# Two-block layer: block transfers on SyncE's queue, y read piece by piece, the keys and values projected in the stage before, the attention loop written out

## The reference, cut to what matters

```
first_block:  h = rmsnorm(x)*(1+scale)+shift;  u = h @ w_in
              y = concat(gated_delta(u[:4128], 8 heads of 128, chunks of 64, both directions),
                         rwkv7(u[4128:], 16 heads of 64, both directions))
              x = rmsnorm(x + gate*(y @ w_out))
second_block: h = x*(1+scale)+shift; q,k,v,g_attn,glu_a,glu_b,g_conv = split(h @ w_in_2)
              y_attn = banded_sink_attention(q,k,v)*silu(g_attn)     # window 128, 16 query, 4 kv heads
              y_conv = conformer_conv(glu_a,glu_b)*silu(g_conv)      # 31 taps deep, depthwise
              x = layer_norm(alpha*x + gate*(concat(y_attn,y_conv) @ w_out_2))
```

## Time and profile before

| | |
|---|---|
| times of three runs | 4370.04, 4384.80, 4388.81 us (median 4384.8) |
| profiled execution | 4372.03 us, span 4370.1 us |
| PE busy | 3557.6 us (81%), mean granted clock 0.902 |
| DVE, ACT, POOL busy | 2135.4, 1060.3, 824.6 us |
| DMA | 375768 packets, 464.6 MB; 230368 packets under 512 B |

### The profile page before, as it was taken

The page is one execution under the profiler, slowest core; times in us unless marked ns, Lnnn a source line. Parts: engine busy times, 40 slices in busy tenths (PEclk is TensorE's granted clock), DMA queues, the critical chain, the costliest instruction groups (busy, mean ns, idle before and its releaser), DMA issues. The chain is left out here.

```text
span 4370.1 us, 54075 instructions
## 1 busy us (share of the span) xinstructions
PE 3557.6 (81%) x19810; PEld 2969.9 (68%) x19810; DVE 2135.4 (49%) x4046; ACT 1060.3 (24%) x1764; POOL 824.6 (19%) x589
## 2 busy tenths in 40 slices
PE   7749999989995877778878777784977787778697
PEld 2238888878885777777777677783766676556385
DVE  0253555555553566566565546664020866681202
ACT  1123555533331112112122112221011221111102
POOL 0000000000000111111111100000655555454173
PEclk9979999999997888889888878887998998889899
DMA  7312443355554444444444322223313111111221
GB/s 275 107 52 76 133 148 121 125 165 160 167 163 119 106 104 106 117 106 110 102 105 117 119 81 89 79 71 124 123 48 130 62 64 58 54 62 58 87 96 67
DMA packets 375768, 464.60 MB, mean 106 GB/s; under 512 B 230368, under 2 KB 276544, under 8 KB 369168
## 3 DMA queue, kind: packets, MB, share of 16 engines
q1 hardware_dynamic: 257376, 363.18, 27.1%
q0 software_dynamic: 20480, 67.13, 5.4%
q10 hardware_dynamic: 97712, 31.61, 3.0%
HBM read 382.80 MB, written 81.63 MB: 106 GB/s over the span
## 5 line engine op out<-in xcount | busy, mean ns | idle before, releaser
L942 PE MATMUL pjl<-high,w_high 128*128 128x512 f32 x960 | 392.8, 409 | 193.8 <-DVE arena L2852 49.0
L925 POOL TENSOR_TENSOR w_high<-ring_o,cst 128x1024 fp32r<-128x1024 f32 x152 | 303.4, 1996 | 566.8 <-PE pjl L944 395.3
L943 PE MATMUL pjl<-low,w_high 128*128 128x512 f32 x960 | 382.7, 399 | 0.0
L944 PE MATMUL pjl<-high,w_low 128*128 128x512 f32 x960 | 382.0, 398 | 0.0
L927 POOL TENSOR_TENSOR w_low<-ring_o,w_high 128x1024 fp32r<-128x1024 f32 x152 | 377.9, 2486 | 11.9
L942 PEld LDWEIGHTS pjl<-high,w_high 128*128 128x128 f32 x960 | 186.5, 194 | 249.0 <-issue 165.6
L1910 POOL DMA_DIRECT2D arena_r<-in_w_ada x256 | 137.8, 538 | 945.5 <-DVE arena_r L2262 794.1
L2842 DVE SCALAR_TENSOR_TENSOR arena<-arena 128x512 f32<-128x512 f32 x232 | 247.8, 1068 | 7.8
L1069 PE MATMUL pjl<-h_high,wh_in 128*128 128x512 f32 x544 | 214.5, 394 | 25.0 <-DVE wl_in L1088 25.0
L1088 DVE TENSOR_TENSOR wl_in<-ring,wh_in 128x1024 fp32r<-128x1024 f32 x136 | 164.2, 1221 | 134.4 <-ACT wh_in L1081 134.3
L1069 PE MATMUL xu<-h_high,wh_in 128*128 128x512 f32 x544 | 219.9, 404 | 0.0
(11 more groups left out here) (449 smaller groups left out, 7930.1 us busy)
## 6 DMA issues: line engine op xcount, KB each, us to landing
ring<-in_w_lr SPq DMA_DIRECT2D x136, 512.0 KB, 4.1
arena_r<-in_w_ada POOLq DMA_DIRECT2D x256, 256.0 KB, 3.3
arena<-in_w_ada SPq DMA_DIRECT2D x32, 1024.0 KB, 6.5
ring_o<-in_w_out SPq DMA_DIRECT2D x64, 512.0 KB, 3.6
ring_o<-in_w SPq DMA_DIRECT2D x64, 512.0 KB, 3.6
arena_r<-rk_d SPq DMA_DIRECT2D x128, 192.0 KB, 3.9
rk_d<-arena_p SPq DMA_DIRECT2D x72, 192.0 KB, 1.9
arena_p<-gate_rows SPq DMA_DIRECT2D x32, 386.0 KB, 6.3
```

The source lines that it names most:

```text
L925: pool.tensor_tensor(h, w, one, ALU.mult).then_inc(S[done + "h"], 1)
L942: pe.matmul(lat, wh[:, c], ah, start=kk == 0, stop=False)
L943: pe.matmul(lat, wh[:, c], al, start=False, stop=False)
L944: last = pe.matmul(lat, wl[:, c], ah, start=False, stop=kk == KT - 1)
```

## The change

Four things, all of them in the order of work; no arithmetic is taken away but a few copies.

1. The hops go from ACT's program to SP's, in both recurrences. `blocks_out` takes 4 squares of 32 x 32 (runs of 128 B) instead of 8 of 16 x 16; `blocks_in` then picks the 16 x 16 blocks out in 4 DMAs of 384 runs of 64 B, where it took 2 of 48 rows of 1 KB. `inverse_out` has 4 DMAs for 2, `inverse_in` 8 as before. The reversing copies go from ACT to DVE. The steps are 5, 5, 5 in slots 4 to 6 of the RWKV stage (4, 4, 4, 3 in 4 to 7) and 3 a slot in slots 6 to 10 of the other (2 a slot in 6 to 11 and 3 in 12). `LATER` puts its 16 sums in other slots.
2. y comes in 8 DMAs, the first weights stand between them on SP, X is loaded after them by SP instead of at once by ACT, and PE's first tile waits for each of its 16 column blocks.
3. The 4 tiles of keys and values stand at the end of `phase_out`, their weights and the first 4 halves of `w_2` come from the same ring there.
4. `phase_two`'s loop is written out; convolution unit 2i+1 is carried into pass i+1, a second buffer `ub` holds it; the waits at the head of a pass are gone; the last unit stands beside the `g_conv` tiles.

```
-LATER = {0: 3, 3: 3, 6: 3, 9: 3, 12: 2, 15: 2}
+LATER = {0: 1, 1: 2, 2: 2, 3: 1, 11: 1, 12: 1, 13: 2, 14: 1, 15: 2, 16: 2, 17: 1}
-R_STEPS = {4: range(0, 4), 5: range(4, 8), 6: range(8, 12), 7: range(12, 15)}
+R_STEPS = {4: range(0, 5), 5: range(5, 10), 6: range(10, 15)}
+def blocks_out(sp, e, S, q, a, LT):
+    for g in range(4):
+        s = slice(32 * g, 32 * g + 32)
+        sp.dma_start(e["lb_d"][:, g].rearrange("u (i j) -> i u j", j=32), LT[s].rearrange("p d u t -> p (d u) t")[:, :, s]).then_inc(S[q + "_h1"], 16)
+def blocks_in(sp, e, S, q, a, LBr, LB):
+    sp.wait_ge(S[q + "_h1"], 64 * a + 64)
+    for d, dst in enumerate((LBr[0:48], LB[64:112])):
+        for h in range(2):
+            s = slice(16 * h, 16 * h + 16)
+            sp.dma_start(dst[24 * h:24 * h + 24].rearrange("p (i j) -> p i j", j=16),
+                         e["lb_d"][6 * d:6 * d + 6].rearrange("u g (i j) -> (u g) i j", j=32)[:, s, s]).then_inc(S[q + "_h2"], 16)
...
             with sp.Fori(0, PAIRS - 1) as i:
+                blocks_there(i * 2 + 1)
                 sp.wait_ge(S["r_oa"], 1 + i * 16)
                 load_set(i, 1)
+                blocks_back(i * 2 + 1)
                 sp.wait_ge(S["r_q"], i * 16 + 14)
                 load_a(i + 1, 0)
+                blocks_there(i * 2 + 2)
                 sp.wait_ge(S["r_oa"], 1 + i * 16 + 4)
                 load_set(i + 1, 0)
                 load_rest(i)
+                blocks_back(i * 2 + 2)
                 sp.wait_ge(S["r_q"], i * 16 + 22)
                 load_a(i + 1, 1)
...
             for m in range(GH):
+                if m + 2 < GH:
+                    sp.wait_ge(S["g_ltc"], 2 * (m + 2) + 2)
+                    blocks_out(sp, e, S, "g", m + 2, LT[m % 2])
+                    blocks_in(sp, e, S, "g", m + 2, LBr, LB)
                 if m + 3 < GH:
                     load_a(m + 3)
...
+            pe.wait_ge(S["o_rt"], 1)
+            for j in range(4):
+                column_tile(pe, e, "o_done", kv_banks[j], half + 2 * KT + 2 * j + 1, None if j else "o_hl")
...
-            with dve.Fori(0, 4) as i:
-                dve.wait_ge(S["n_y"], 1 + i * 2)
-                dve.wait_ge(S["n_cv"], 1 + i * 2)
...
+                if i:
+                    conv(u - 1, 0, 4)
+                    gate(i - 1, 1)
+                    conv(u - 1, 4, 18)
+                rows(i, 0)
+                norm(i, 0)
+                if i:
+                    conv(u - 1, 18, 26)
+                rows(i, 1)
+                norm(i, 1)
+                if i:
+                    conv(u - 1, 26, 31)
+                unit(u)
+                conv(u, 0, 12)
+                rows(i, 2)
+                norm(i, 2)
+                conv(u, 12, 18)
+                rows(i, 3)
+                norm(i, 3)
+                unit(u + 1)
+                conv(u, 18, 23)
+                gate(i, 0)
+                conv(u, 23, 31)
```

More of the change, by code:

```diff
@@ L477 @@
 G_VALUES, G_KEYS = 13, 14
-G_STEPS = {6 + n: range(2 * n, 2 * n + 2) for n in range(6)} | {12: range(12, 15)}
-G_DONE = 13
+G_STEPS = {6 + n: range(3 * n, 3 * n + 3) for n in range(5)}
+G_TURNED, G_DONE = 6, 10
 def phase_gdn(nc, e):
@@ L553, in _ @@
             load_c(0)
+            hops(0)
             load_a(1)
+            hops(1)
             load_a(2)
@@ L2379, in _, with weights @@
             pool.memset(unused[:, 1:2], 0.0).then_inc(S["o_done"], DONE)
-            split_weights(pool, e, "o_done", loads(half), 0, 2 * KT)
+            split_weights(pool, e, "o_done", loads(half), 0, 2 * KT + 8)
         @block.sync
         def _(sp):
-            for q in range(4):
-                sp.dma_start(whole[:, 4 * q:4 * q + 4], ydram[4 * q:4 * q + 4].rearrange("k p t -> p k t")).then_inc(S["o_y"], 16)
-            stream(sp, e, io["w_out"], half, KT)
+            def weights(src, at, s):
+                sp.wait_ge(w_used, at - RING + s + 1)
+                sp.dma_start(ring[:, s], src[s // 2, :, s % 2 * HK:s % 2 * HK + HK]).then_inc(w_loaded[s], 16)
+            weights(io["w_out"], half, 0)
+            for q in range(8):
+                sp.dma_start(whole[:, 2 * q:2 * q + 2], ydram[2 * q:2 * q + 2].rearrange("k p t -> p k t")).then_inc(S[f"o_y{q}"], 16)
+                if q == 1:
+                    weights(io["w_out"], half, 1)
+            weights(io["w_out"], half, 2)
+            weights(io["w_out"], half, 3)
+            sp.dma_start(X[:, 0:4], io["xT"][:, 0:4]).then_inc(S["o_x"], 16)
+            sp.dma_start(X[:, 4:KT], io["xT"][:, 4:KT]).then_inc(S["o_xx"], 16)
+            stream(sp, e, io["w_out"], half, KT, 1)
+            stream(sp, e, io["w_kv"], half + 2 * KT, 4)
+            for s in range(RING):
+                weights(io["w_2"], half + 2 * KT + 8, s)
         @block.scalar
@@ L2561, in _ @@
             P0 = pj[0][:, 0:LAT]
-            for j in range(4):
-                if j:
-                    pe.wait_ge(S["n_kv"], j)
-                column_tile(pe, e, "n_done", P0, half + 2 * j + 1)
             pe.wait_ge(S["n_kv"], 4)
@@ L2572, in _ @@
             last.then_inc(S["n_vt"], 1)
-            pe.wait_ge(S["n_dup"], 64)
-            pe.wait_ge(S["n_kv"], 6)
-            with pe.Fori(0, 4) as i:
+            for i in range(4):
                 tiles = [0]
@@ L2604, in values @@
                     pe.wait_ge(S["n_pt"], i * 8 + 2 * h + 2)
+                    if i and not h:
+                        pe.wait_ge(S["n_at"], i * 2)
                     hs = slice(64 * (h % 2), 64 * (h % 2) + 64)
@@ L2873, in _, with product @@
+            conv(7, 0, 4)
+            gate(3, 1)
+            dve.memset(eps[:], 1e-5).then_inc(S["n_v0"], 1)
+            def product(k):
+                dve.wait_ge(S["z_g"], 1 + k + 1)
+                dve.tensor_tensor(gcv[:, k], graw[:, 0], graw[:, 1], ALU.mult).then_inc(S["z_gm"], 1)
+            conv(7, 4, 14)
+            product(0)
+            conv(7, 14, 23)
+            product(1)
+            conv(7, 23, 31)
+            for k in range(2, 8):
+                product(k)
             dve.wait_ge(S["n_cv"], 1 + 8)
```

286 lines of the change are left out of this document (137 added, 149 removed).

## The result

The changed kernel takes 4145.3 us in the median of four runs (4143.3 to 4150.4); beside it the kernel before took 4377.4. The ratio is 0.9475 (95% interval 0.9438 to 0.9512). The profiled execution took 4150.4 us with a span of 4148.6, against 4370.1 before; the difference of the spans, 221.5 us, is what the following ledger splits. PE's share of the span goes from 81% to 85% (the page's first row: busy us of each engine).

A forecast was written before the change was run, and what follows sets the result against it. PE was busiest, but in the RWKV stage the chain between engines was taken as the bound. Terms -90 - 20 - 17 - 23 - 83 = -233 took 4372 to 4139, 4145 for the median; range 4065 to 4240.

The forecast's parts named there:

- The term for the wait before L2007: RWKV stage: an earlier inverse, fetched without a load beside it, saves PE about 7.5 us a half, -60 us.
- ACT's copies: RWKV stage: copies no longer stand behind 8 DMA issues; about two thirds of PE's 31.3 us before L1992 go, -20.
- sums of w_ada now stand in slots 13 to 17 beside the scan: +7: RWKV stage: a cost of 7 us for sums that now share those slots with the scan.
- +1: RWKV stage: cost in us a unit if the blocks' fetch in short runs lands late, from a possible 0 to 10.
- The clock's term: RWKV stage: 0.43 us of clock loss for each idle us of PE; 66 us fewer stops give another -24.
- Rival 1: Hops stay late through SP's queue and short runs; both recurrences gain 15 us in place of 110: 4240 us, chance 0.15.
- the formula: Second block: (L - 37) (0.65/2.3 + 0.35/0.75) = 62 taps, with POOL working 80 us of a pass of L.
- The lower bound of 115 us a pass: Second block: PE gets by with 115 us, as in the first pass; the block's gain would be -107.
- Rivals 1, 2 and 5: Second: POOL's port makes passes 137 us, 4187 to 4200, chance 0.12. Fifth: a gate or ACT's copy holds PE, 4215, 0.05.
- rival 4: More than forecast: passes of 115 us and twice the clock given back in the RWKV stage: 4070 us, chance 0.08.
- Rival 3: Recurrences: DVE waits for fetched blocks before its first step, 10 us a unit in 24 units: 4490 us, chance 0.04.
- no wait of DVE at its first step above 2 us: RWKV stage: a sign named in advance that would show the forecast mechanism in the changed kernel.

The follow-up runs named there:

- old-sums kernel: The changed kernel with only the old slots of the `w_ada` sums put back, steps and hops unchanged: 4181.3 us, ratio 0.957 to the kernel before.

## Why the prediction was right, and where it was not

The time, the direction and the sum hold: -233 forecast for the profiled execution, -221.5 of span measured. That the median of 4145.3 us meets the forecast of 4145 to a fraction of a us is luck: the sum missed by 12 us, and the 6 us added for the median went the wrong way, since the profiled execution stood 5 us above it. By its steps:

- **RWKV stage, -90 against -91.5, but not by the steps given.** The term for the wait before L2007 is right: 60 forecast, 55.8 measured. ACT's copies were mis-sized on the low side (-20 against -31 before L1992's successors, and another 25 before L2053 that the sum left out). **The step that failed is "sums of w_ada now stand in slots 13 to 17 beside the scan: +7".** Moving them is worth -31 us of the stage: the old table put up to three of them ahead of DVE's copy for PE, and PE's stop there goes from 43.6 us before to 10.3, and back to 53.1 in the old-sums kernel. The prediction looked at where the sums go and not at what they leave. Against that stands the second error, the fetched blocks. The prediction takes "+1" a unit for them but has it in no term of its sum; DVE waits 3.8 us a unit, and PE stops 78 us behind it. The errors are large and opposite, and that they cancel is luck. In all, PE's idle time fell by 52 us against the 66 of the terms. The clock's term was -24 (0.43 times 66 is 28), and PE's busy time fell by 39.5. A half has 18 slots, not 15, so a slot is about 3.8 us; that changes little.
- **What a late fetch costs.** The fear of the short runs, for which the Trainium skill ("DMA: Bandwidth & Descriptors", Specifications: 512 B as the smallest transfer at line rate) was brought, is hardly borne out here: whole rows of 1 KB in their place land 0.6 us a unit sooner in the median, their four more issues take it back, and the wait is 84.8 us where it was 80.8. The 8.1 us of the way are issues and two landings one behind the other. Rival 1's 13.0 us for a fetch did not come back either: with SP's load behind them the 8 DMAs of an inverse take at most 7.7 us to L2268.
- **Gated-delta stage, -20 against -27.9.** The stop before L607 went as said. L659's wait kept 25.9 of its 28.8 us, in six longer ones, against -7. The costs at the stage's start and of a crowded DVE (+12) did not show; its table is worth 2 us. The unchanged stage of the kernel with new RWKV tables took 529.1 us, so 6 of the 8 us of surplus are within what two traces differ by.
- **Output stage, -17 against -12.9.** The new stop was forecast in its place, about 15 us for the first square, and is 17.78. From the end of `low` the bias way takes 32.6 us instead of 26.9: its first two transfers take 6.3 and 16.8 us beside X and the weights, where they took 1.5 and 12.4, and the third is 3.4 us shorter. Taking the way off the path gives 18.5 us in the stage.
- **Keys and values, -23 against -24.8.** As worked out.
- **Second block, -83 against -66.7.** The mechanism was right, the size a little off: passes of 126.2 us, not 123. The taps take 62 times 1.347, 83.5 us, what the formula gave for L = 120; DVE's other work is 30 us, not 27, and its waits are 12, not 10. The tail won 16 us, not 21. The reading of a tap as slowed to about 2.3 us fully beside POOL gives the right price for the wrong reason: a tap that meets an operation of POOL's is held until it ends. Of the eight taps in 11.42 us five took 0.75 us and three 2.3 to 2.8, not four and four at 2.1. The rule of the Trainium skill ("SBUF — State Buffer", Who interferes with whom) holds: 75 taps are held by POOL's reading operations instead of 41. But it is not the carry that does most of this, as the kernel without it shows by 68. The accumulator in PSUM shows the cause with POOL's work untouched, and agrees with the same section, which exempts a DVE instruction with at most one input in SBUF. The lower bound of 115 us a pass was wrong: it was the first pass, which has the stop of 4.3 us for DVE in it and a lower clock; PE gets by with 109.7.
- **Rivals and signs.** Rivals 1, 2 and 5 did not come, and rival 4's passes only with the accumulator in PSUM. Rival 3's mechanism did, at 3.8 us a unit in the RWKV stage and none in the other, under the 5 us from which it would have decided. Of the signs, one failed clearly: no wait of DVE at its first step above 2 us. Eleven of the 15 halves after the first have one of 3.4 to 5.2 us.

What stays open: whether a shorter way for the blocks (issues from two queues, for one) would bring PE's 78 us back. Moving the steps behind the state's update moved the stop to the next copy, and filling the wait made it no shorter; the way itself was not shortened.

## What to carry to other kernels

When work moves off a slot, read what stood behind it there before pricing where it goes: leaving their old slots took 33 us of PE's stops away, and the new ones cost some 15, at a pair's start. When work fills an engine's idle time beside another engine, look at its operands: one operand moved to PSUM was worth more (65 us) than the carry (49). A way through DRAM that only a later phase needs belongs behind the first thing that a nearer phase waits for.
